# One of eight z units computed in quarters in the passage into a delta-rule recurrence, with the loads, splits and copies around it rearranged

## The reference, cut to what matters

```python
proj = h @ w_in                       # q, k, v, z, b, a, ... ; z is 1024 wide, 8 heads of 128
qc, kc, vc = silu(conv(q, k, v))      # then q and k normalised per head
# per chunk of the recurrence (the reference solves it, forward and backward):
a   = eye + beta * (k @ k.T) * decay  # lower triangular
sol = solve_triangular(a, [v * beta, k * beta * exp(g)])
S   = S * exp(g_last) + k_dec.T @ v_new ; o = q_dec @ S + qk @ v_new
o = rmsnorm(o_fwd + o_bwd) * silu(z)
```

## Time and profile before

| what | value |
|---|---|
| median of 3 runs | 1656.18 us (1656.0 to 1656.58) |
| the profiled execution | 1656.19 us, span from first to last instruction 1654.4 us |
| TensorE busy | 1628.2 us, 98% of the span |
| VectorE, ScalarE, GpSimd busy | 817.0, 700.3, 905.4 us |
| mean granted TensorE clock | 0.995 |

### The profile page before, as it was taken

One profiled execution on the slowest core, in us unless ns is written; L12 is line 12 of the kernel. 1 busy time (PEld: TensorE's weight loads), 2 busy tenths in 40 slices (PEclk: granted clock), 3 DMA queues, 4 the chain that ended last, 5 costly groups with the idle time before them and its releaser, 6 DMA issues.

```text
span 1654.4 us, 23617 instructions
## 1 busy us (share of the span) xinstructions
PE 1628.2 (98%) x9479; PEld 1397.9 (84%) x9479; DVE 817.0 (49%) x1322; ACT 700.3 (42%) x1048; POOL 905.4 (55%) x515
## 2 busy tenths in 40 slices
PE   7999989999999999999999999999999999999998
PEld 7999978889998888888888888888887888888887
DVE  7778955734343001232121131128999862457744
ACT  6666554333233223233322333336543453366652
POOL 3455654333356445545555554449977666456661
PEclk9999999999999999999999999999999999999999
DMA  5586388565322343322332333332232423333332
GB/s 205 154 262 188 90 266 261 146 193 159 117 84 90 102 142 101 96 95 91 100 100 91 103 91 113 102 102 90 101 96 83 124 85 98 91 101 102 102 97 81
DMA packets 122357, 202.47 MB, mean 122 GB/s; under 512 B 32624, under 2 KB 73736, under 8 KB 122248
## 3 DMA queue, kind: packets, MB, share of 16 engines
q1 hardware_dynamic: 119912, 197.46, 38.4%
q10 hardware_dynamic: 2336, 3.51, 0.6%
HBM read 170.97 MB, written 29.97 MB: 121 GB/s over the span
## 4 chain that ended last, share of the span: by engine, by line
PE 86%; DVE 8%; ACT 2%; issue 1%; POOL 1%; DMA 1%; SPq 0%; DVEq 0%; ACTq 0%; POOLq 0%
PE ps L433 75%; PE ps L1922 3%; DVE cacc L2418 3%; DVE inv L665 1%; DVE prd L662 1%; PE ps L973 1%; PE ps L994 1%; PE ps L987 1%; PE ps L998 1%; PE ps L981 1%; POOL hp L2782 1%; DMA d_p<-dec 0%; PE ps L940 0%; PE ps L959 0%; PE ps L1587 0%
## 5 line engine op out<-in xcount | busy, mean ns | idle before, releaser
L421 POOL TENSOR_TENSOR w_lo<-w_raw,w_hi 128x1024 fp32r<-128x1024 f32 x264 | 634.0, 2410 | 426.7 <-ACT w_hi L415 414.0
L433 PE MATMUL ps<-hp,w_hi 128*128 128x512 f32 (+2 forms) x2432 | 594.4, 344 | 0.0
L433 PEld LDWEIGHTS ps<-hp,w_hi 128*128 128x128 f32 x2432 | 401.1, 188 | 53.6 <-issue 2.3
L433 PE MATMUL ps<-hp,w_lo 128*128 128x512 f32 (+2 forms) x1216 | 370.2, 342 | 0.0
L415 ACT ACTIVATE w_hi<-w_raw 128x1024 fp32r<-128x1024 f32 x264 | 277.3, 1054 | 140.8 <-DMA w_raw<-in_w 133.1
L433 PEld LDWEIGHTS ps<-hp,w_lo 128*128 128x128 f32 x1216 | 210.6, 188 | 26.1
L433 PE MATMUL ps<-n_hi,w_hi 128*128 128x512 f32 x464 | 184.1, 397 | 0.0
L433 PE MATMUL ps<-n_hi,w_lo 128*128 128x512 f32 x464 | 180.7, 389 | 0.0
L433 PE MATMUL ps<-n_lo,w_hi 128*128 128x512 f32 x464 | 180.5, 389 | 0.0
L1356 DVE SCALAR_TENSOR_TENSOR ps<-u_in,par,ps 128x511 f32<-128x511 f32 (+14 forms) x210 | 154.6, 739 | 6.5
L433 PEld LDWEIGHTS ps<-n_hi,w_hi 128*128 128x128 f32 x464 | 87.1, 188 | 19.8 <-issue 1.9
(11 more groups left out here) (431 smaller groups left out, 2612.4 us busy)
## 6 DMA issues: line engine op xcount, KB each, us to landing
w_raw<-in_w SPq DMA_DIRECT2D x264, 512.0 KB, 3.5
d_y<-zero SPq DMA_DIRECT2D x6, 688.0 KB, 6.0
d_x<-zero SPq DMA_DIRECT2D x6, 688.0 KB, 6.1
d_at<-at SPq DMA_DIRECT2D x16, 256.0 KB, 3.3
d_kc<-kc SPq DMA_DIRECT2D x16, 256.0 KB, 3.3
d_qd<-eg SPq DMA_DIRECT2D x16, 256.0 KB, 3.2
d_p<-dec SPq DMA_DIRECT2D x16, 256.0 KB, 3.4
AT<-d_at SPq DMA_DIRECT2D x16, 256.0 KB, 6.6
```

Of the source, the lines that this page charges most:

```text
L421: e.tensor_tensor(w_lo[:, u % RAW, :], w_raw[:, u % RAW, :], w_hi[:, u % RAW, :].bitcast(F32), ALU.subtract).then_inc(s_lo, 1)
L433: mm = e.matmul(ov, w, r[:, k, t0:t1], start=(first and n == 0 and p3 == 0), stop=(last and n == len(tiles) - 1 and p3 == 2))
```

## The change

- z1 is taken out of slots 0 and 1 and computed in four quarters of six products (`pe_z_quarter`) in the passage: after the transposes of v, after the meta transposes, after pair 4's products, and after slot 0's `pe_yx`. It goes to bank 3, and `act_z_copy` copies it out. z2 goes to slots 0 and 1, z3 to slots 2 and 3, the first half of z4 to the end of slot 3. Slot 3 holds two halves where it held four; slots 4 and 5 are as before.
- In the passage the last v head and the scaled meta rows are copied by VectorE (`dve_vt`, `dve_msa`) and no longer by ScalarE, the exponentials of pair 4 are taken apart (`act_eg`, `act_de`) and moved behind the copies that TensorE waits for, and `pe_msa` and `pe_pk` change places with the first inverse steps. z2 is rounded and split in the passage.
- Roundings of z3 and z4 now stand in ScalarE's steps 0 and 1, the split of z3 in GpSimd's step 0, of z4 in step 1, of z5 in step 3. In slots 0, 1 and 3 ScalarE's `act_xc` comes ahead of them.
- SyncE loads one z unit a step: z4, z5, z6, z7 in steps 0 to 3 (`ZLOAD`), where step 2 had none and step 3 two.
- `AT` and `X` are loaded with the 96 rows that are used, not 128.
- `pe_yx` makes only the one block of X that is used and not two (12 products for 16), and `act_xc` copies one block.

The diff, cut to its core:

```diff
--- before.py
+++ after.py
@@ -99,15 +99,17 @@
         22: [("vt", 2), ("msa", 0)], 23: [("vtm", 2), ("msb", 0)],
-        24: [("z", 0), ("pgp", 4), ("pgq", 4), ("vt", 3), ("pkp", 4), ("vtm", 3)]}
+        24: [("z", 0), ("pgp", 4), ("vt", 3), ("zq", 0), ("eg", 4), ("vtm", 3), ("zq", 1)]}
...
 PREP = {0: 5, 1: 6, 2: 7}
-ZAT = {3: 2, 4: 4, 5: 6}
-ZBANK = [5, 4, 4, 6, 7, 4, 6, 7]
+ZAT = {4: 4, 5: 6}
+ZBANK = [5, 3, 4, 4, 7, 6, 4, 7]
+ZLOAD = {0: (4,), 1: (5,), 2: (6,), 3: (7,), 4: (8, 9), 5: (10, 11)}
+ZSPLIT = {0: (3,), 1: (4,), 3: (5,), 4: (6, 7), 5: (8, 9)}
 SCA = {6: 0, 8: 1, 10: 2, 12: 3, 14: 4}
@@ -767,12 +780,18 @@
                     e.wait_ge(s_pK[0][d], 64)
-            for i in range(2):
+            for i in range(1 if p == 3 else 2):
                 h = 2 * p + i
...
                 v.then_inc(m_vte.sem, 1)
+
+        def dve_vt(e):
+            e.wait_ge(*m_vt.at(7))
+            for c in range(NCH):
+                v = e.tensor_scalar(v_tok[:, 1, c, 3, :], ps[:, 5, c * P:(c + 1) * P], nk[:, c + 1, 7:8], None, ALU.mult)
+            v.then_inc(dg.sem, 1)
@@ -888,6 +907,10 @@
+        def dve_msa(e):
+            e.wait_ge(*m_mw.at(2))
+            e.tensor_tensor(v_met[0:META, HG:H, :], bankv(MSA[1], META, P), cell(b2, META, 0, HG, HG, P), ALU.mult).then_inc(m_mv.sem, 1)
+
         def act_msb(e, hf):
@@ -947,8 +970,9 @@
                     r = quad(i)
-                    e.matmul(half_cols(LB[s], 0)[quad(j), u], T[r, u, 0:BLK], Y[r, u, r], start=True, stop=True)
-                    mm = e.matmul(half_cols(LB[s], 1)[r, u], Y[r, u, r], T[r, u, 0:BLK], start=True, stop=True)
+                    mm = e.matmul(half_cols(LB[s], 0)[quad(j), u], T[r, u, 0:BLK], Y[r, u, r], start=True, stop=True)
+                    if (i, j) == pairs32(s)[s]:
+                        mm = e.matmul(half_cols(LB[s], 1)[r, u], Y[r, u, r], T[r, u, 0:BLK], start=True, stop=True)
             mm.then_inc(q_yx[s].sem, 1)
@@ -1014,9 +1038,8 @@
             e.wait_ge(*q_yx[s].at(k))
-            for i, j in pairs32(s):
-                m = e.activation(SQ[s]["X"][quad(i), :, quad(j)], half_cols(LB[s], 1)[quad(i)], ACT.Copy, scale=-1.0)
-            m.then_inc(q_xc[s].sem, 1)
+            i, j = pairs32(s)[s]
+            e.activation(SQ[s]["X"][quad(i), :, quad(j)], half_cols(LB[s], 1)[quad(i)], ACT.Copy, scale=-1.0).then_inc(q_xc[s].sem, 1)
@@ -1105,10 +1128,11 @@
                 e.wait_ge(s_pA[1][1], 64)
-            e.dma_start(SQ[s]["AT"][:], unit_rows(d_at, hf, slot)).then_inc(s_ld["AT"][s], 16)
+            r = used_rows(s)
+            e.dma_start(SQ[s]["AT"][r], unit_rows(d_at, hf, slot, r)).then_inc(s_ld["AT"][s], 16)
             if k % 4 == 0:
                 e.wait_ge(s_sca[hf], 64)
-            e.dma_start(SQ[s]["X"][:], unit_rows(d_x, hf, slot)).then_inc(s_ld["X"][s], 16)
+            e.dma_start(SQ[s]["X"][r], unit_rows(d_x, hf, slot, r)).then_inc(s_ld["X"][s], 16)
             if k:
@@ -1147,31 +1167,39 @@
             if half is FIRST:
-                if j == 1:
+                if j == 2:
                     e.wait_ge(*m_vme.at(3))
-                elif j == 2:
-                    e.wait_ge(*ev.at("z", 2))
-                elif j in (3, 4):
+                elif j == 3:
+                    e.wait_ge(*ev.at("z", 3))
+                elif j in (4, 5):
                     e.wait_ge(*m_p.at(15))
-                elif j >= 5:
-                    e.wait_ge(*ev.at("z", (3, 4, 5)[j - 5]))
+                elif j >= 6:
+                    e.wait_ge(*ev.at("z", j - 2))
             mm = gemm(e, BASE["z"] + j, [ps[:, ZBANK[j], :]], TOK, h_hi, h_lo, half, half is FIRST, half is SECOND)
...
             round_unit(e, BASE["z"] + j + 2)
-            if j == 2:
+            if j == 3:
                 e.wait_ge(*m_qd.at(15))
...
                 e.activation(zs(1), z_1[:], ACT.Silu)
+                e.activation(zs(2), z_2[:], ACT.Silu)
             e.wait_ge(s_pe, BASE["z"] + j + 1)
...
-        def act_z_second(e):
-            e.wait_ge(s_pe, BASE["z"] + 2)
-            e.activation(z_1[:], ps[:, ZBANK[1], :], ACT.Copy).then_inc(ev.sem, 1)
+        def pe_z_quarter(e, i):
+            if i == 0:
+                e.wait_ge(*cv.at("t", 4 * 24))
+            mm = gemm(e, BASE["z"] + 1, [ps[:, ZBANK[1], :]], TOK, h_hi, h_lo, K8[2 * i:2 * i + 2], i == 0, i == 3)
+            if i == 3:
+                mm.then_inc(s_pe, 1)
+
+        def act_z_copy(e, j):
+            e.wait_ge(s_pe, BASE["z"] + j + 1)
+            e.activation((z_1, z_2)[j - 1][:], ps[:, ZBANK[j], :], ACT.Copy).then_inc(ev.sem, 1)
@@ -1566,6 +1594,8 @@
                     sp_chain(e, *SLOTS[q + 2])
+                for j in ZLOAD.get(q, ()):
+                    load_unit(e, BASE["z"] + j)
                 for u in units_at(q):
@@ -1671,10 +1703,13 @@
+            pe_msa(e, 1)
+            pe_pk(e, 4)
+            pe_z_quarter(e, 2)
             pe_t(e, 0, 0, 32)
-            pe_msa(e, 1)
+            pe_msb(e, 1)
             pe_yx(e, 0, 0)
-            pe_msb(e, 1)
+            pe_z_quarter(e, 3)
             pe_t(e, 0, 0, 64)
@@ -1685,9 +1720,9 @@
                 if q in (0, 1):
-                    pe_z(e, 1, (FIRST, SECOND)[q])
-                if q == 2:
-                    pe_z(e, 2, FIRST)
+                    pe_z(e, 2, (FIRST, SECOND)[q])
+                if q in (2, 3):
+                    pe_z(e, 3, (FIRST, SECOND)[q - 2])
                 if q in ZAT:
@@ -1702,6 +1737,8 @@
                     pe_yx(e, *nx)
+                if q == 3:
+                    pe_z(e, 4, FIRST)
                 if q in ZAT:
@@ -2042,18 +2080,22 @@
                         act_silu(n)
-                    if task in ("pg", "pgq"):
                         act_pg(e, arg)
+                    if task == "eg":
+                        act_eg(e, arg, 0)
                     if task == "qs":
...
+            act_de(e, 4, 0)
+            act_eg(e, 4, 1)
+            act_de(e, 4, 1)
             act_tc(e, 0, 0, 32)
-            act_msa(e, 1)
+            act_msb(e, 1)
             act_xc(e, 0, 0)
-            act_msb(e, 1)
             act_tc(e, 0, 0, 64)
+            act_z_copy(e, 1)
             for q, (s, k) in enumerate(SLOTS):
@@ -2069,17 +2111,21 @@
                     act_pg(e, PREP[q])
+                if q < 2 or q == 3:
+                    act_xc(e, *nx)
                 if q < 2:
-                    round_unit(e, BASE["z"] + q + 2)
+                    round_unit(e, BASE["z"] + q + 3)
                 if q == 1:
-                    act_z_second(e)
+                    act_z_copy(e, 2)
+                if q == 3:
+                    act_z(e, 3)
                 if q in ZAT:
...
                     round_unit(e, BASE["sc"] + 3 * SCB[q] + 4)
-                if nx:
+                if q == 2 or 4 <= q < 15:
                     act_xc(e, *nx)
@@ -2449,6 +2495,8 @@
             dve_pg(e, 4)
+            dve_vt(e)
+            dve_msa(e)
             dve_yc32(e, 0, 0)
@@ -2477,7 +2525,7 @@
                     dve_pk(e, PREP[q])
-                if q in ZAT:
+                if q in (3, 4, 5):
                     sub_part(e, 1, 3 * q - 9)
@@ -2804,18 +2852,21 @@
+            split_unit(e, BASE["z"] + 2)
             e.wait_ge(*m_vtm.at(3))
...
                 if q == 4:
-                    e.wait_ge(*ev.at("z", 3))
+                    e.wait_ge(*ev.at("z", 4))
                     e.memset(oT[:, HG:H, :], 0.0).then_inc(pz.sem, 1)
...
                     pool_pk(e, PREP[q])
+                for j in ZSPLIT.get(q, ()):
+                    split_unit(e, BASE["z"] + j)
                 for u in units_at(q):
```

More of the change, by code:

```diff
@@ L229, in build @@
         SQ = [{n: z(f"{n}{s}", [P, HG, P], places[2 * i + s]) for i, n in enumerate(("AT", "X", "Y", "TR", "PT", "QD", "KC", "KD", "VN"))} for s in range(2)]
-        z_0, z_1 = z("z_0", [P, SEQ], 8192), z("z_1", [P, SEQ], 10240)
+        z_0, z_1, z_2 = (z(f"z_{j}", [P, SEQ], 8192 + 2048 * j) for j in range(3))
         zs_b = [z("zs0", [P, HG, SEQ], 25344), z("zs1", [P, HG, SEQ], 42240)]
@@ L265, in build, with unit_rows, used_rows @@
         d_qn = dram("d_qn", (2, P, SEQ))
-        def unit_rows(t, hf, slot):
-            return bass.AP(tensor=t, offset=(hf * 8 + slot) * HG * USTEP, ap=[[P, P], [USTEP, HG], [1, P]])
+        def unit_rows(t, hf, slot, rows=slice(0, P)):
+            return bass.AP(tensor=t, offset=(hf * 8 + slot) * HG * USTEP + P * rows.start, ap=[[P, rows.stop - rows.start], [USTEP, HG], [1, P]])
+        def used_rows(s):
+            return slice(BLK, P) if s else slice(0, P - BLK)
         def unit_blocks(t, hf, slot, n):
@@ L369, in build @@
         dp = Signal(sem("s_dp"), p=sum(j // 2 + 3 if j < 4 else 1 for j in range(KT)))
-        dg = Signal(sem("s_dg"), halo=9, n2=1, zero=1, wlo=1, b=1, ch=20, gr=1, lam=18, g2=2)
+        dg = Signal(sem("s_dg"), halo=9, n2=1, zero=1, wlo=1, b=1, ch=20, gr=1, vt=1, lam=18, g2=2)
         zr = Signal(sem("s_zr"), sc=2, bval=5)
```

(29 more changed lines are left out.)

## The result

| | before | after |
|---|---|---|
| median of 13 runs | 1656.58 us (1655.93 to 1661.01) | 1661.14 us (1659.62 to 1664.04) |
| the profiled execution | 1656.19 us, span 1654.4 | 1661.36 us, span 1659.4 |

The account below looks back on a forecast made before the run. TensorE, busy for 98% of the span, was taken as the bound, with full DMA queues limiting the gain before slot 5. 2.35 us at slot 5 plus 0.2 for `pe_yx` off 1656.19 gave 1653.6 us, range 1649.5 to 1656.6.

Parts of the forecast that it names:

- The passage: Before slot 0: z1's quarters fill TensorE's idle time almost free; slot 0 starts at 219.0 against 218.90.
- Slot 0, stores decide: VectorE's second `dec` waits for pair 4's store, landing 0.8 us earlier; slot 1 starts near 231.5, 2.0 us earlier.
- Slot 1's new wait on ScalarE: ScalarE, rounding z4 in step 1, stands for its load; TensorE waits 2.1 us at slot 2's `pe_y64`.
- If TensorE stays full, the clock should not fall: After the passage: no half clock, so slot 0's opening saves at most 1.7 us in all.
- The rival that named it: Clock falls in the new waits before slot 5: 3.25 us for 6.5 us at half clock, 1656.9 us; chance 0.1.
- The gather, forecast at 266.5: Slot 2 keeps its work, so the gather, waiting for pair 7's stores, moves from 267.48 to 266.5.
- Slot 3 shorter by 5.69 us: Slot 3 holds two z halves instead of four, saving TensorE 5.69 us.
- z6 ahead of AT and X: z6's load ahead of slot 5's AT and X delays them 1.5 us; bounds 0 and 2.1.
- The rival that z6's load hides: z6's load costs nothing; slot 5's `pe_t` runs at 275.4, total 1651.4 us; chance 0.25.
- The 96 rows save a quarter of two transfers: AT and X of slot 5: fewer rows save 0.35 us of DMA time; bounds 0 and 0.4.
- `pe_yx` 0.02 us a slot: 12 products for 16 save 0.02 us a slot over 11 slots, 0.2 us; bounds 0 and 0.1 a slot.
- Slot 5's `pe_t`, forecast at 277.65: It runs when X lands, at 277.65 instead of 280.01, 2.35 us earlier.

Follow-up runs that it names:

- e1: Changed kernel with ScalarE's rounding of z4 moved behind slot 2's copies; 1660.4 us, ratio 1.0015 to the kernel before.
- e6: Changed kernel with AT and X loaded in 128 rows again; 1658.79 us, ratio 1.0006 to the kernel before.
- e8: Changed kernel with idle products filling three TensorE waits, one in slot 2 and two in slot 4; 1659.27 us, ratio 1.0009 to the kernel before.
- e4: Changed kernel with idle products filling two TensorE waits, one in slot 2 and one in slot 4; 1660.83 us, ratio 1.0016 to the kernel before.
- e2: Changed kernel with z6's load back in step 3, behind AT and X of slot 5; 1658.64 us, ratio 1.0 to the kernel before.
- e12: Kernel before with one edit, AT and X loaded in 96 rows instead of 128; 1657.85 us, ratio 0.9999 to the kernel before.
- e14: Changed kernel with AT and X loaded in 112 rows instead of 96; 1662.68 us, ratio 1.0029 to the kernel before.
- e15: Kernel before with AT and X loaded in 112 rows instead of 128; 1658.1 us, ratio 0.9999 to the kernel before.
- e9: Changed kernel with z4 to z6 loaded behind the next slot's AT, X, Y, z4 rounded in step 2, slot 4's chain loads before the gather; 1654.54 us, ratio 0.9984.
- e10: Changed kernel with z4 to z6 loaded behind AT, X, Y, z4 rounded later, slot 4's chain loads before the gather, and 128-row loads; 1654.45 us, ratio 0.9979.

## Why the prediction was wrong

Before's clock differs from after's by 1.65 us, the difference of the v transposes; "on before's clock" adds it.

- **The passage: right.** z1's quarters run without a gap at clock 1.00, slot 0's opening takes 1.16 us. Slot 0 starts at 219.6 on before's clock, forecast 219.0.
- **Slot 0, stores decide: right, a little small.** `dec` waits 0.41 us for the store and runs 0.5 us earlier than before, for 0.8. Slot 1 starts at 232.2, forecast 231.5.
- **Slot 1's new wait on ScalarE: right in place and cause, too small.** z4's load was issued 0.8 us earlier than before, as worked out. It was given 6.3 us to land and took 7.8: the term mis-sized is this landing. The wait was 3.06 us, forecast 2.1. e1 shows the cause. In e6, with 128 rows, the same load takes 6.1 us and the wait is 1.26, so the rows are the part that was missing.
- **"If TensorE stays full, the clock should not fall": the step that failed.** It was argued for the passage and silently kept for slots 2 to 5, although the same forecast put a wait of 2.1 us into slot 2 and two more into slot 4. The rival that named it priced one fall, behind slot 4, at a chance of 0.1. It fell twice, about 6.8 us at 0.50 each, 3 us or a little more a time. The Trainium skill, "TensorE: Matmul & The Clock Gate", "What's actually happening", says "the default state is throttled, and activity releases the throttle"; this trace agrees: 0.50 from the end of each of the two long waits, and 1.00 again after some 6 us of products. What it cost in the end is measured by e8: roughly 2.3 us of 3.8. The sum had 0 for it.
- **The fall in slot 2 was passed on to the transfers.** It made slot 2's stores late. The gather, forecast at 266.5, was issued at 269.6 on before's clock, 3.1 us later. Counted from the v transposes that is 62.8 us, against 60.8 in e4 and 60.9 in e8, which keep the wait and lose the fall: 2.0 of the 3.1 us are the clock, the rest is the longer wait. TensorE was then late enough that KC cost 1.15 us and not 2.1: one error hid part of another.
- **Slot 3 shorter by 5.69 us: right.** From slot 3's start to slot 4's it is 13.8 us with 1.15 of waiting, before 18.0: 5.4 less.
- **z6 ahead of AT and X: about right with 128 rows, too small with 96.** With 128 rows X of slot 5 took 5.7 us for 4.7 before (e6): 1.0 for the forecast's 1.5. With 96 rows it took 8.0 with z6's load ahead and 5.4 without it (e2): 2.7, beyond the upper bound of 2.1. The rival that z6's load hides is wrong.
- **"The 96 rows save a quarter of two transfers": wrong in sign.** Forecast −0.35 us; in its place X took 8.0 us for 5.7 with 128 rows, and the unit ahead 7.1 for 4.8: about 2 us later. Without z6's load ahead the rows cost X of slot 5 only 0.6 us (e12: 5.3 for 4.7), so the two edits to the queue were dearer together than the sum priced them one by one. The bounds, 0 to 0.4 us of saving, left out a loss, because the cost was taken as bytes by throughput. The Trainium skill, "SBUF — State Buffer", "Door 1: The DMA port swizzle", would give a saving of 0, which is nearer but no loss either; the measurement decides. Why fewer rows are slower these runs don't show; e14 and e15 show that 112 rows do it as well, and the last section says where the time goes.
- **`pe_yx` 0.02 us a slot: right.** The group takes 0.45 us, before 0.46.

Slot 5's `pe_t`, forecast at 277.65, ran at 283.6 on before's clock, 5.9 us late. X of slot 5 was issued at 275.5 where the forecast's working gives 272.3: 3.2 us, from slot 2's late stores (272.3 is 272.82 less 1.0, and 0.47 for issuing z6's load). It took 8.0 us to land where the forecast left 5.35: 2.65 us, 2.3 of them the rows (e6). Against before that `pe_t` is 3.6 us later, and with the 3 us of the second fall behind it this is the 6.4 us by which slot 6 and all after it are late.

## What to carry to other kernels

A wait that a forecast puts on TensorE is to be priced twice: once as the wait, and once as half clock that may follow it, and then again at every transfer that the slowed products feed. Two waits that hold the same path are to be cured together: here the ratios say 1.3 and 3.8 us alone, 6.5 together, and only the pair made the kernel faster than before. And in a full DMA queue the bytes of a transfer aren't its price: before a load is cut to the rows that are used, its neighbours' landings are to be measured.

## What was not expected of the hardware

**Fewer rows land later.** With the queue full, joined loads of 96 or 112 rows of 512-byte pieces made the unit ahead of them land 9.2 to 10.5 us after the same store, for 8.7 to 8.9 us with 128 rows. The DMA engines don't idle meanwhile (their share is 1.07 to 1.14 from 8 to 12 us after that store with 128 rows, 1.13 to 1.20 with fewer), each small packet takes longer: by the packets' own times in the traces, a 512-byte packet takes 29 to 30 ns on average in that stretch in the three kernels with 128 rows of the table, and 36 to 43 ns in the eleven with fewer. In e9 and e10, whose AT and X are served sooner, it is 36 and 28 ns from 4 to 8 us. So 96 rows at 40 ns take as much of the engines as 128 at 30, and 112 rows at 41 to 43 ns take more. Why a packet takes longer is open.

**The same instructions fall or don't fall in clock.** In the changed kernel and the kernels made from it the clock fell behind every one of the eleven waits of 2.1 us or more in slots 1 to 5, behind three of the five between 1.4 and 2.0 us (1.44, 1.51 and 1.95, but not 1.50 and another of 1.51), and behind none that was shorter. Yet a short wait is not safe. All kernels hold a wait of 1.2 us near 66 us, in code that no edit touches. Windows from 70 to 76 us of the kernel before and of the changed one:

```profile
70.00:76.00 6.00, 6.00 (x53) 5.60 (x46) 0.69 (x1) 4.47 (x7) 2.40 (x1) 0.84 0.01 3
```

```profile
70.00:76.00 6.00, 6.00 (x51) 6.00 (x49) 0.69 (x1) 4.07 (x8) 2.38 (x1) 1.00 0.00 0
```

Of 16 traces one, the changed kernel's, shows no fall there; the others are at 0.50 for about 3 to 7 us, and the v transposes start anywhere from 205.1 to 209.0 us. Between the two executions shown the same products are already 1.6 us apart at 72 us, so that is nearly the whole of the offset of 1.65 above. It is probably much of the spread of the runs as well, whose traces weren't kept: two profiled executions are to be compared from a common instruction behind it.
